# Cross-attention scores for 64 queries at a time, and RG-LRU gate products as 64x64 quadrant products

## The reference

```
proj = rmsnorm(x, norm_g) @ w_in            # q, k, v, gate | lru_x, lru_gate | xa_q, xa_gate
sb_out  = stick_breaking_attention(q, k, v)             # 8 heads x 64
xc      = causal_depthwise_conv(lru_x, conv_w, conv_b)  # 256 channels
r = sigmoid(einsum('bsnd,nde->bsne', xb, w_rg) + b_rg)  # 4 channel blocks of 64x64
i = sigmoid(einsum('bsnd,nde->bsne', xb, w_ig) + b_ig)
lru_out = scan(exp(-8 r softplus(-lam)), sqrt(1-a^2) * i * xc)
scores  = rmsnorm(xq) @ rmsnorm(mk)^T / 8               # 4 heads x 64, 256 memory rows
xa_out  = softmax(scores) @ mv
out = x + concat(sb_out*silu, lru_out*silu, xa_out*silu) @ w_out
```

## Time and profile before

| what | value |
|---|---|
| runs, median (lowest to highest) | 1555.12 us (1554.22 to 1555.98) |
| span of the profiled execution | 1551.8 us |
| the runs' median above that span | 3.3 us |
| PE busy | 1506.0 us, 97% |
| ACT busy | 878.3 us, 57% |
| DVE busy | 1040.6 us, 67% |
| chain that ended last | PE 85% |
| mean granted TensorE clock | 0.995 of full speed |

### The profile page before, as it was taken

One profiled execution on the slowest core, in us unless ns is written; L12 is line 12 of the kernel. 1 busy time (PEld: TensorE's weight loads), 2 busy tenths in 40 slices (PEclk: granted clock), 3 DMA queues, 4 the chain that ended last, 5 costly groups with the idle time before them and its releaser, 6 DMA issues.

```text
span 1551.8 us, 29770 instructions
## 1 busy us (share of the span) xinstructions
PE 1506.0 (97%) x10764; PEld 732.2 (47%) x10764; DVE 1040.6 (67%) x1907; ACT 878.3 (57%) x1593; POOL 318.3 (21%) x305
## 2 busy tenths in 40 slices
PE   4999999999999999999999999999999999999996
PEld 2444444444444444444444444444444444444452
DVE  6988766676666676666666665667666667666674
ACT  6887555565446565445566445566545556544661
POOL 3222111222211222212222211222211122221120
PEclk9999999999999999999999999999999999999998
DMA  9545665545655545555545556454555454565645
GB/s 364 197 126 103 155 131 111 118 115 133 145 124 120 119 116 126 142 122 128 130 105 122 138 125 145 109 117 114 134 140 131 115 118 116 128 145 123 124 95 137
DMA packets 443336, 205.83 MB, mean 133 GB/s; under 512 B 412000, under 2 KB 412448, under 8 KB 442144
## 3 DMA queue, kind: packets, MB, share of 16 engines
q1 hardware_dynamic: 443008, 205.18, 54.8%
q10 hardware_dynamic: 288, 0.13, 0.0%
HBM read 55.53 MB, written 50.53 MB: 68 GB/s over the span
## 4 chain that ended last, share of the span: by engine, by line
PE 85%; SPq 2%; ACT 2%; DMA 1%; issue 1%; DVE 1%; ACTq 0%; DVEq 0%
PE bank L1816 26%; PE bank L1818 25%; PE bank L1817 25%; PE bank L1900 2%; SPq L495 2%; PE bank L2014 2%; PE bank L1864 2%; PE bank L1885 1%; PE bank L1909 1%; DMA x_lo<-x_t 0%; PE bank L1953 0%; PE bank L1948 0%; PE bank L1950 0%; PE bank L1949 0%; ACT fail_and_take L1047 0%
## 5 line engine op out<-in xcount | busy, mean ns | idle before, releaser
L1816 PE MATMUL bank<-w_pair,x_hi 128*128 128x512 f16 x1528 | 581.6, 381 | 9.4 <-DVE w_pair L1248 5.2
L1818 PE MATMUL bank<-w_pair,x_lo 128*128 128x512 f16 x1528 | 580.6, 380 | 0.0
L1817 PE MATMUL bank<-w_pair,x_hi 128*128 128x512 f16 x1528 | 580.5, 380 | 0.0
L1143 ACT ACTIVATE spare<-xy,columns 128x1024 f16<-128x1024 f32 x32 | 36.8, 1149 | 395.4 <-DVE columns L1674 395.4
L1816 PEld LDWEIGHTS bank<-w_pair,x_hi 128*128 128x128 f16 x1528 | 149.7, 98 | 183.4 <-issue 6.9
L1818 PEld LDWEIGHTS bank<-w_pair,x_lo 128*128 128x128 f16 x1528 | 149.8, 98 | 181.4 <-issue 1.9
L1817 PEld LDWEIGHTS bank<-w_pair,x_hi 128*128 128x128 f16 x1528 | 149.9, 98 | 166.8 <-issue 2.7
L1816 PE MATMUL bank<-wo_pair,y_hi 128*128 128x512 f16 x480 | 181.9, 379 | 0.8 <-issue 0.8
L752 POOL TENSOR_TENSOR fail_and_take<-fail_and_take,seen 128x512 f32<-128x512 f32 x32 | 42.5, 1327 | 680.9 <-ACT fail_and_take L904 680.9
L1817 PE MATMUL bank<-wo_pair,y_hi 128*128 128x512 f16 x480 | 181.9, 379 | 0.0
L1818 PE MATMUL bank<-wo_pair,y_lo 128*128 128x512 f16 x480 | 181.9, 379 | 0.0
(11 more groups left out here) (271 smaller groups left out, 2398.3 us busy)
## 6 DMA issues: line engine op xcount, KB each, us to landing
xy<-in_x SPq DMA_DIRECT2D x32, 512.0 KB, 3.6
spare<-in_x SPq DMA_DIRECT2D x31, 512.0 KB, 4.1
out<-spare SPq DMA_DIRECT2D x30, 512.0 KB, 2.9
gate_kept<-gate SPq DMA_DIRECT2D x32, 256.0 KB, 2.2
v_kept<-v_sb SPq DMA_DIRECT2D x32, 256.0 KB, 2.1
fail_and_take<-v_sb SPq DMA_DIRECT2D x64, 128.0 KB, 2.4
q_kept<-q_t SPq DMA_DIRECT2D x32, 256.0 KB, 3.9
k_kept<-k_t SPq DMA_DIRECT2D x32, 256.0 KB, 4.4
```

The lines of the kernel that those rows point to most:

```text
L1143: act.activation(y_halves[:, 0, :], xy[:, :], ACT.Copy, scale=y_top[:, :]).then_inc(s["y_high"], 1)
L1816: pe.matmul(dst, hi[:, k, :], pair[:, 0, k, :], start=k == 0, stop=False)
L1817: pe.matmul(dst, hi[:, k, :], pair[:, 1, k, :], start=False, stop=False)
L1818: last = pe.matmul(dst, lo[:, k, :], pair[:, 0, k, :], start=False, stop=k == KD - 1)
```

## The change

Three parts of the program change, all inside step n:

- `memory_scores` takes the 128 queries as two halves of 64. Each of its 12 products (64 rows by 128 weight columns, 256 moving columns) becomes two of 64 by 64. Nothing else about them changes; the banks stay.
- `gate_products` takes no longer four f32 products of 128x128 but eight of 64x64, leaving out the zero blocks. The rg products write the partitions of their own channels and the ig products the other half of the partitions, so that the four products of one channel half lie on four quadrants of the array. Row half 0 writes SMALL (or SCORE[0] for d = 0), row half 1 writes HEADS (or SCORE[1]).
- `gate_sigmoids` reads eight pieces of 64 partitions by 128 columns instead of four of 128 by 128. The pieces of ig move to the other half of the partitions while they are read. The bias of ig is laid out with its halves swapped on the host.

The heads' product, which writes HEADS, now also waits for the gates to be read. Two waits on PE also count in `passed`.

```
+        def gate_banks(d):
+            return (SMALL, HEADS) if d else SCORE
+        def other_half(odd):
+            return slice((1 - odd) * HD, (2 - odd) * HD)
@@ gate_sigmoids, on ACT
-                    for g, (dst, bias) in enumerate(((rec_g, brg), (in_g, big))):
-                        for h in range(LH):
-                            at = (g * LH + h) * P
-                            last = act.activation(dst[:, h, :], (SCORE[0], SMALL)[d][:, at:at + P], ACT.Sigmoid,
-                                                  bias=bias[:, h:h + 1])
+                    for h in range(LH):
+                        for odd in range(2):
+                            r, to = slice(odd * HD, (odd + 1) * HD), other_half(odd)
+                            at = gate_banks(d)[odd]
+                            act.activation(rec_g[r, h, :], at[r, h * P:(h + 1) * P], ACT.Sigmoid, bias=brg[r, h:h + 1])
+                            last = act.activation(in_g[r, h, :], at[to, h * P:(h + 1) * P], ACT.Sigmoid,
+                                                  bias=big[to, h:h + 1])
@@ memory_scores, on PE
-                        have(pe, s["sig"], n - 1)
+                        have(pe, s["sig"], n - 1, ahead_of_loop=True)
-                            for odd in range(2):
-                                r = slice(odd * HD, (odd + 1) * HD)
-                                last = pe.matmul((TURN, SCORE)[d][odd][:, c * NM:(c + 1) * NM], xq_t[r, a, c, :],
-                                                 mk_t[r, b, c, :], start=a + b == 0, stop=a == 1)
+                            for top in (0, HALF):
+                                for odd in range(2):
+                                    r = slice(odd * HD, (odd + 1) * HD)
+                                    last = pe.matmul((TURN, SCORE)[d][odd][top:top + HALF, c * NM:(c + 1) * NM],
+                                                     xq_t[r, a, c, top:top + HALF], mk_t[r, b, c, :],
+                                                     start=a + b == 0, stop=a == 1)
@@ gate_products, on PE
-                    have(pe, s["y_mixed"], n - 2)
+                    have(pe, s["y_mixed"], n - 2, ahead_of_loop=True)
-                    for g, by_head in enumerate((rg_blocks, ig_blocks)):
-                        for h in range(LH):
-                            at = (g * LH + h) * P
-                            last = pe.matmul((SCORE[0], SMALL)[d][:, at:at + P], by_head[:, h, :], xc[:, h, :],
-                                             start=True, stop=True)
+                    for h in range(LH):
+                        for by_head, turn_over in ((rg_blocks, False), (ig_blocks, True)):
+                            for odd in range(2):
+                                r = slice(odd * HD, (odd + 1) * HD)
+                                to = other_half(odd) if turn_over else r
+                                last = pe.matmul(gate_banks(d)[odd][to, h * P:(h + 1) * P], by_head[r, h, r], xc[r, h, :],
+                                                 start=True, stop=True)
@@ before the heads' product, on PE
                     have_turned(pe, w_turned, n - 1)
+                    have(pe, s["gates_read"], n - 1)
@@ laid_out, on the host: b_ig goes in with the two halves of each 128 channels swapped
```

More of the change, by code:

```diff
@@ L2122, in laid_out @@
         "per_partition": np.concatenate([columns(i["norm_g"][0]), columns(i["mem_g"][0]), taps] + [
-            columns(i[n][0]) for n in ("conv_b", "b_rg", "b_ig", "lru_lambda")] + [
+            columns(v) for v in (i["conv_b"][0], i["b_rg"][0], i["b_ig"][0].reshape(-1, 2, P // 2)[:, ::-1].reshape(-1),
+                                 i["lru_lambda"][0])] + [
             twice(i[n][0]) for n in ("sb_q_g", "sb_k_g", "xa_q_g", "xa_k_g")], axis=1),
```

## The result

The changed kernel takes 1599.48 us (median, 1598.48 to 1601.02) against 1554.67 us for the kernel before on the same chip, a ratio of 1.0287 with a 95% interval from 1.0274 to 1.0299. The forecast was 1571 us with a range of 1563 to 1580. The direction was right; the loss, 44.8 us, is almost three times the 15.8 us forecast, and lies outside the range.

What follows compares the result with a forecast made beforehand. PE was taken to bound the kernel, the chain ACT, SP, `x_lo` close behind. 25 steps gave 10.8 us, four early steps 4.0, the last steps 1.0: 15.8, span 1567.6, plus 3.3, say 1571 us; range 1563 to 1580.

Steps and rivals of the forecast that it cites:

- What bounds the kernel, and who passes a delay on: PE ends last; the chain ACT, SP, `x_lo` has 0.57 us slack, so 1.00 us on ACT costs 0.43 per loop step.
- PE's uncertain term: Time of PE's gate products, -0.5 to +0.8 us per step; said to be covered up to +0.43 us by the wait at `project(0)`.
- ACT's share: Gate sigmoids: eight pieces of 64 partitions at 0.25 us each, 2.0 us in all, +1.00 us in the step.
- four early steps: Steps before 312 us, where the landing of `x_lo` already ends or nearly ends PE's wait: +1.00 us each, 4.0 us.
- the middle one: PE's gate products: second f32 passes hold back the next product, 1.0 us, nothing won; the ends were -0.5 and +0.8 us.
- Memory scores at nothing: Memory scores on PE: -0.1 us for the shape change that goes, +0.1 for leaving 64x64 behind the gates, no net change.
- The nearer waits: Waits on the same delay before `project(0)`: output product, slack 1.04 us, wait up to 0.2; heads' product for `gates_read`, harmless.
- The faster one: First rival: sigmoids on 64 partitions cost half and four quadrants run side by side, 0.5 us saved per step, 1539 us; 5%.
- The second: Rival: ACT's pieces are cheap but PE's gate passes queue in order, nothing changes, 1555 us; 4%.
- the fourth: Rival: the 16 f32 gate passes do not overlap at all, PE loses 0.8 us per step, 1580 us; 7%.
- The third: Rival: sigmoids cost 1.00 us more, SP makes up time, only the output product's wait binds, some 0.15 us a step, 1560 us; 6%.
- The signs of being wrong: In the trace after: sigmoids closer than 0.19 us, a gap in SP's queue between `q_t` and `x_lo`, or a shorter step.

Runs made afterwards that it cites:

- four sigmoids more: Kernel before with four more whole sigmoids, their output overwritten unread, in front of the four in all steps but step 1: 1572.59 us, ratio 1.0114.
- pieces sorted: Kernel before with its four sigmoids cut into eight of 64 partitions, the four lower halves first, then the four upper: 1579.03 us, ratio 1.0156.
- changed, grouped: Changed kernel with its eight sigmoids reordered so that those of one kind and half stand next to each other: 1583.39 us, ratio 1.0182.
- pieces in turn: Kernel before with each of its four sigmoids cut into two of 64 partitions, lower and upper half in turn: 1603.78 us, ratio 1.0315.
- The two sorted runs: The runs "pieces sorted", made from the kernel before, 1579.03 us, and "changed, grouped", made from the changed kernel, 1583.39 us.
- that with POOL's copies: Changed kernel with rec_g and in_g in separate banks, four sigmoids of 128 partitions, POOL copying in_g's exchanged halves back: 1544.34 us, run again 1544.58 us.
- run with the order changed: Kernel with four sigmoids of 128 partitions and POOL copying in_g's halves back, the two gate products of one quadrant now adjacent: 1546.98 us, ratio 0.9944.
- whole sigmoids: Changed kernel's products read by four sigmoids of 128 partitions: 1543.81 us with gate values mixed up, 1544.34 us with POOL putting in_g's halves back.

## Why the prediction was wrong, step by step

**What bounds the kernel, and who passes a delay on: right.** That `x_lo` arrives 0.57 us before it decides, and that ACT and SP hand on a delay whole, can be tested at five doses, that is delays of five sizes. The period is that of the loop, 46.13 us before, from the first memory score of one step to that of the next over 23 steps.

| kernel | ACT late, us | period, us | longer by | ACT late less that | time less before, us |
|---|---|---|---|---|---|
| four sigmoids more | 1.05 | 46.61 | 0.48 | 0.57 | 17.3 |
| pieces sorted | 1.26 | 46.82 | 0.69 | 0.57 | 24.3 |
| changed, grouped | 1.37 | 46.93 | 0.80 | 0.57 | 28.7 |
| changed kernel | 1.84 | 47.39 | 1.26 | 0.58 | 44.8 |
| pieces in turn | 2.01 | 47.58 | 1.45 | 0.56 | 48.5 |

The slack is 0.56 to 0.58 us at every dose, whether PE's stay is 1.76 or 1.22 us. That also shows the sentence that the wait covers PE's uncertain term: PE's 0.54 us bought nothing in the changed kernel.

**The failed step: ACT's share.** The prediction put a piece of 64 partitions "at worst" at 0.25 us, "+1.00 us in the step". The pieces cost 0.375 each, 3.00 us in all, +1.84. The upper bound was no bound: it held for a row of instructions that all use the same partitions and so overlap (0.35 long, 0.25 apart), and in the changed order each of the seven neighbours changes the half that is read or written. The two sorted runs show it by taking changes away. Put into the forecast's own sum, the right size gives 25 x (1.84 - 0.57) = 31.8, 1.84 in each of the four early steps, 7.4, and 1.84 at the tail: 41.0 us, 1596 instead of 1571. A bound from both sides should have reached up to the duration in the row, 0.35 to 0.37 us, as what a piece costs when nothing overlaps: 8 x 0.36 = 2.9 us, nearly what was measured.

**What the corrected sum leaves open: 3.8 of 44.8 us.** Step 1 was put at 0, since ACT waits 1.30 us for DVE there. That wait did swallow its part: `heads_high` ends 18.28 us behind the first memory score of step 1 instead of 17.76, 0.5 us late and not 1.84. The start of the 24 periods is 10.3 us late. The four early steps make 7.6 of it (3.3, 2.2, 0.9 and 1.1, where 4 x 1.84 is 7.4; in the first of them `x_lo` also goes out 0.9 us later behind `heads_high` and lands 0.6 us later behind its issue), the first of the 25 steps 1.4, and step 1 itself is 1.7 us longer, from 43.31 to 45.00, with its first memory score 0.3 us earlier. How much of step 1's is ACT's cannot be said: without work added on ACT there other variants took 43.1 to 44.5, and one kernel, that with POOL's copies, 44.44 and 43.30 in its two traces. The end is 4.0 us longer where the sum has 1.84, and there too variants with nothing added on ACT differ among themselves by 2.7 us. What the open 3.8 us are is not shown.

**PE's share.** "I take the middle one", passes in order and nothing won, was wrong. The gates come in four rounds of 0.109 us, the end of -0.5 us, measured -0.54 with the scores. It cost the forecast nothing, as that text said itself, since PE waits anyway. The Trainium skill, TensorE: Matmul & The Clock Gate, Part 3, "The mechanism", says that matmuls start and end strictly in program order. The run with the order changed does not agree, with all 16 passes started within 0.41 us, and a stay of 1.29 us, for two products, four passes, in a row on each quadrant; the measurement decides. The records do not name the quadrant of a pass, so the order within one is not seen.

**Memory scores at nothing.** -0.1 and +0.1 for the changes of shape: in front of the old gates +0.02, in front of quadrant gates -0.14. The balance was right for neither alone.

**The nearer waits: one was missed.** The prediction looked at the output product, and put up to 0.2 us there. It did not look at `project(5)`, which waits for the reading of `project(3)` by ACT and DVE. ACT came 1.84 us later and PE 0.54 earlier, and counted from start to start PE loses 1.56 us there, the mean of 23 steps of the loop (1.47 to 1.65), so 1.84 + 0.54 - 1.56 = 0.82 us were to spare. The other four doses of the table, with 0.24, 0.45, 1.08 and 1.20 us lost there, give 0.81 to 0.83. It adds nothing to the step: PE loses 47.39 - (46.13 - 0.54) = 1.80 us in it, 1.56 here and the other 0.24 at `x_lo`, which sets the total. But it means that moving `x_lo` up in SP's queue alone would have won, by estimate, at most that 0.24 us of the 1.26 that a step lost; no run tried it. The wait for `gates_read` was harmless, as said.

**The rivals.** The faster one asked for two things. The four quadrants side by side came true, the half-price sigmoid did not, and the latter decided. Its 1539 us is near what whole sigmoids give, 1544. The second and the fourth fall with the passes side by side. The third falls with SP's queue, which made up nothing: `x_lo` goes out 12.9 us behind the end of `heads_high` in the loop, before as after. The signs of being wrong that the prediction named all lay on the fast side or in SP's queue, and none of them came; sigmoids further apart than 0.25 us were not among them, and those were what came. The Trainium skill's rule, ScalarE: Activation LUTs, "What ACT_TABLE_LOAD costs", one element per cycle in each lane, agrees with a piece of half the partitions lasting as long as a whole one, 0.35 us in both. The estimate of 0.29 us per instruction, from that section's figures, lies between the 0.25 and 0.375 measured here; that the overlap of neighbours hangs on their partitions was seen only in the runs.

## What to carry to other kernels

Cutting ACT's sigmoids along the partitions saved it nothing: a piece lasts as long as the whole. Where neighbours then lay in different halves they lost their overlap as well, so bound such a piece by its full duration, not by the distance of undisturbed ones, and if pieces are needed, sort them by half. Choose the layout of PE's output so that the reader takes it whole, and leave the exchange of halves to an engine with idle time. Here a second chain had only 0.57 us to spare beside PE's: it turned 1.84 us on ACT into 1.26 in every step, and made PE's gain worthless. Read the slack of such a chain first, and of every wait on the same delay: the next one was only 0.24 us behind.

## What the runs showed of the hardware

- An ACT sigmoid of 128 columns from PSUM lasts 0.35 to 0.38 us on 64 or 128 partitions in the steps shown. Starts stand 0.25 to 0.27 us apart where neighbours read and write the same partitions, 0.36 to 0.38 where the half read or the half written changes. A change of the PSUM bank or of the tile written adds nothing.
- f32 passes of 64x64 by 128 columns run four at a time in rounds of 0.109 us, two at a time where only two quadrants have work (eight rounds). A pass for a free quadrant does not stand behind one for a busy quadrant: four in a row per quadrant cost 0.07 us in 16 passes (run with the order changed).
- Going from 64x64 scores to 128x128 f32 products costs 0.02 us more than from 64x128 scores, and to 64x64 products 0.08 us less (0.68 against 0.76 us to the first gate pass).
- POOL copies 64x256 f32 to the other half of the partitions in 0.64 to 0.82 us in the step shown.
